# The order of high and low matmuls inside a unit: grouped for most columns, five orders for gate and up

## The reference

```python
# first block
proj = h @ w_in                      # mixer: SSD part, short convolution part
... @ w_out
q = (h @ w_q); k, v = mem_n @ w_k, mem_n @ w_v; ... @ w_o
(jax.nn.silu(h @ w_gate) * (h @ w_up)) @ w_down          # D_FF = 5632
# second block
p = h @ w_in[i]                      # pool, hyena and gated mixers
... @ w_out[i]
up = dwconv3(h @ ffn_w_up[i], ...); gate, val = jnp.split(up, 2, axis=-1)
x = x + (jax.nn.silu(gate) * val) @ ffn_w_down[i]
```

## Time and profile before

| | |
|---|---|
| median of 3 runs | 2719.59 us |
| profiled execution | 2724.14 us, of which the span of instructions 2722.4 us |
| TensorE busy | 2656.2 us, 98% of the span |
| VectorE, ScalarE busy | 1924.6 us, 1495.8 us |
| granted TensorE clock, mean | 0.992 |
| memory traffic | 490.76 MB, mean 180 GB/s |

### The profile page before, as it was taken

How to read it: one execution, slowest core, us unless ns; L and a number is a source line. 1 busy time by engine, 2 the same in 40 slices (tenths; PEclk the granted TensorE clock), 3 DMA queues, 4 the chain that set the end, 5 groups by cost and what they waited for, 6 DMA issues and landing times.

```text
span 2722.4 us, 38546 instructions
## 1 busy us (share of the span) xinstructions
PE 2656.2 (98%) x14978; PEld 2286.7 (84%) x14978; DVE 1924.6 (71%) x2916; ACT 1495.8 (55%) x2307; POOL 388.7 (14%) x391
## 2 busy tenths in 40 slices
PE   7999999999998999999999999999999999999997
PEld 7888888888887888888888878888888888888886
DVE  8776777777787665656565679687876767676775
ACT  6555566768555444444444456545555555555554
POOL 3011100403411000010101033011101010101012
PEclk9999999999998999999999999999999999999998
DMA  6555566656554555666666656536566666666663
GB/s 247 173 180 182 184 191 193 186 182 183 174 175 134 168 162 171 186 187 188 189 186 187 190 161 209 162 124 185 178 193 188 187 189 189 186 187 187 190 178 118
DMA packets 135838, 490.76 MB, mean 180 GB/s; under 512 B 15207, under 2 KB 15528, under 8 KB 135656
## 3 DMA queue, kind: packets, MB, share of 16 engines
q1 hardware_dynamic: 135656, 488.31, 59.2%
HBM read 486.12 MB, written 2.13 MB: 179 GB/s over the span
## 4 chain that ended last, share of the span: by engine, by line
PE 87%; DVE 8%; ACT 2%; issue 2%; DMA 0%; DVEq 0%; ACTq 0%; SPq 0%
PE ps L715 32%; PE ps L733 24%; PE ps L716 16%; PE ps L730 12%; DVE wl L1218 3%; ACT wh L936 1%; DVE hT L1218 1%; DVE X L1224 1%; PE ps L872 0%; PE ps L905 0%; DVE A L1224 0%; DVE T L1224 0%; DVE R L1218 0%; DVE Gf L1218 0%; DVE T L1218 0%
## 5 line engine op out<-in xcount | busy, mean ns | idle before, releaser
L1218 DVE TENSOR_TENSOR wl<-raw,wh 128x1024 fp32r<-128x1024 f32 x902 | 1139.7, 1268 | 723.9 <-ACT wh L936 722.6
L936 ACT ACTIVATE wh<-raw 128x1024 fp32r<-128x1024 f32 x902 | 952.4, 1059 | 967.2 <-PE ps L716 536.2
L733 PE MATMUL ps<-X,wh 128*128 128x512 f32 x2816 | 860.1, 396 | 2.8 <-DVE hT L1218 2.8
L715 PE MATMUL ps<-XG,wh 128*128 128x512 f32 x2304 | 827.3, 403 | 29.7 <-DVE hT L1218 16.4
L715 PE MATMUL ps<-X,wh 128*128 128x512 f32 x2032 | 725.2, 401 | 2.0 <-DVE wl L1218 1.3
L716 PE MATMUL ps<-XG,wl 128*128 128x256 f32 x2304 | 650.4, 282 | 0.0
L716 PE MATMUL ps<-X,wl 128*128 128x256 f32 x2032 | 568.7, 280 | 0.0
L730 PE MATMUL ps<-X,wl 128*128 128x256 f32 x2816 | 564.6, 281 | 0.0
L715 PEld LDWEIGHTS ps<-XG,wh 128*128 128x128 f32 x2304 | 436.8, 190 | 142.9 <-DVE hT L1218 21.8
L733 PEld LDWEIGHTS ps<-X,wh 128*128 128x128 f32 x2816 | 481.5, 189 | 71.9 <-issue 4.7
L730 PEld LDWEIGHTS ps<-X,wl 128*128 128x128 f32 x2816 | 484.6, 189 | 61.5
(11 more groups left out here) (172 smaller groups left out, 1313.6 us busy)
## 6 DMA issues: line engine op xcount, KB each, us to landing
raw<-in_w_gate SPq DMA_DIRECT2D x176, 512.0 KB, 3.7
raw<-in_w_down SPq DMA_DIRECT2D x176, 512.0 KB, 3.7
raw<-in_w_sc SPq DMA_DIRECT2D x96, 512.0 KB, 4.2
raw<-in_w_up SPq DMA_DIRECT2D x88, 512.0 KB, 3.7
raw<-in_w_val SPq DMA_DIRECT2D x88, 512.0 KB, 3.7
raw<-in_w_zx SPq DMA_DIRECT2D x80, 512.0 KB, 3.8
raw<-in_w_in SPq DMA_DIRECT2D x68, 512.0 KB, 3.8
raw<-in_w_osc SPq DMA_DIRECT2D x32, 512.0 KB, 3.7
```

The costliest lines, as they stand in the source:

```text
L715: e.matmul(bank(c, i)[:, :], W1, x, start=st and kk == 0, stop=False)
L733: t = e.matmul(bank(c, i)[:, :], wh[:, b0:b0 + 128], X[:, kx * 512:kx * 512 + 512], start=st and kk == 0, stop=sp and n == ends[i])
L936: return e.activation(out, in_, ACT.Copy, scale=scale)
L1218: return e.tensor_tensor(out, a, b, op)
```

## The change

The code that orders matmuls is written anew. Columns other than gate and up: for each k tile H for i = 0 and 1, then L for i = 0 and 1 (the v columns as before). Gate and up: `ORDERS` becomes the function `orders(which, first)`, picked by the same string of digits. Its five orders are: 0, the grouped H H L L, which was index 1's; 1, H and L in turn all through, each L on the other output tile than the H before it, first H(0) with L(1) and, from the middle, H(1) with L(0) (the first unit of a column starts with H H L, since each bank has to be begun by an H); 2, H(0) H(1) L(1) L(0) for each k; 3, for two k tiles each H H L H L H L L; 4, H H L, then H and L in turn, and an L last. Gate and up units wait for each of their four X tiles instead of once for the last, all ahead of the unit's first matmul. The other engines are as before.

```diff
--- before.py
+++ after.py
@@ -383,14 +383,25 @@
     return at
 
 
-
-ORDERS = [
-    [(k, i, m) for k in range(4) for i in range(2) for m in range(2)],
-    [(k, i, m) for k in range(4) for m in range(2) for i in range(2)],
-    [(k, i, m) for k in range(4) for i, m in ((0, 0), (0, 1), (1, 0), (1, 1))[:2] + (((1, 0), (1, 1)) if k == 0 else ((1, 1), (1, 0)))],
-    [(k, i, m) for m in range(2) for k in range(4) for i in range(2)],
-    [(k, i, m) for q in range(2) for m in range(2) for k in (2 * q, 2 * q + 1) for i in range(2)],
-]
+def orders(which, first):
+
+
+    if which == 0:
+        return [(k, i, m) for k in range(4) for m in range(2) for i in range(2)]
+    if which == 1:
+        head = [(0, 0, 0), (0, 1, 0), (0, 1, 1)] if first else [(0, 0, 0), (0, 1, 1)]
+        mid = [(0, 0, 1)] if first else [(0, 1, 0), (0, 0, 1)]
+        return (head + [(k, i, i) for k in range(1, 4) for i in range(2)] + mid +
+                [(k, 1 - m, m) for k in range(1, 4) for m in range(2)])
+    if which == 2:
+        return [(k, i, m) for k in range(4) for i, m in ((0, 0), (1, 0), (1, 1), (0, 1))]
+    if which == 3:
+        return [(k, i, m) for k in (0, 2) for k, i, m in ((k, 0, 0), (k, 1, 0), (k, 0, 1), (k + 1, 0, 0), (k, 1, 1), (k + 1, 1, 0),
+                                                         (k + 1, 0, 1), (k + 1, 1, 1))]
+    return [(0, 0, 0), (0, 1, 0), (0, 0, 1)] + [(k - (i and m), i, m) for k in range(1, 4) for i, m in (
+        (0, 0), (1, 1), (1, 0), (0, 1))] + [(3, 1, 1)]
+
+
 ORDER_OF = [int(d) for d in "0123401324" "0214303142" "10432042" "0123412034" "431021"]
 
 PLAN = schedule()
@@ -703,25 +714,26 @@
             st, sp = u == c.first, u == c.last
             for kk in range(c.kn):
                 X, kx, s, n = xtile(c, g * c.kn + kk)
-                if kk == 0 or c.kind not in ("gate", "up"):
-                    w.wait_ge(s, xtile(c, g * c.kn + c.kn - 1)[3] if c.kind in ("gate", "up") else n)
-                x = X[:, kx * 512:(kx + 1) * 512]
+                w.wait_ge(s, n)
                 if c.kind in ("gate", "up"):
                     continue
-                for i in range(nb):
-                    b0 = (u % NW) * UN + kk * c.w
-                    if c.kind != "v":
-                        W1, W2 = wh[:, b0 + 128 * i:b0 + 128 * i + 128], wl[:, b0 + 128 * i:b0 + 128 * i + 128]
-                        e.matmul(bank(c, i)[:, :], W1, x, start=st and kk == 0, stop=False)
-                        t = e.matmul(bank(c, i)[:, 0:256], W2, x[:, 0:256], start=False, stop=sp and kk == c.kn - 1)
-                    else:
-                        W1, W2 = wh[:, b0:b0 + 256], wl[:, b0:b0 + 256]
+                x = X[:, kx * 512:(kx + 1) * 512]
+                b0 = (u % NW) * UN + kk * c.w
+                if c.kind == "v":
+                    W1, W2 = wh[:, b0:b0 + 256], wl[:, b0:b0 + 256]
+                    for i in range(2):
                         xh, xl = x[:, i * 128:i * 128 + 128], x[:, 256 + i * 128:384 + i * 128]
                         e.matmul(bank(c, i)[:, 0:256], xh, W1, start=st and kk == 0, stop=False)
                         e.matmul(bank(c, i)[:, 0:256], xh, W2, start=False, stop=False)
                         t = e.matmul(bank(c, i)[:, 0:256], xl, W1, start=False, stop=sp and kk == c.kn - 1)
+                else:
+                    for i in range(nb):
+                        e.matmul(bank(c, i)[:, :], wh[:, b0 + 128 * i:b0 + 128 * i + 128], x, start=st and kk == 0, stop=False)
+                    for i in range(nb):
+                        t = e.matmul(bank(c, i)[:, 0:256], wl[:, b0 + 128 * i:b0 + 128 * i + 128], x[:, 0:256], start=False,
+                                     stop=sp and kk == c.kn - 1)
             if c.kind in ("gate", "up"):
-                order = ORDERS[ORDER_OF[c.i]]
+                order = orders(ORDER_OF[c.i], st)
                 ends = {i: n for n, (kk, i, low) in enumerate(order)}
                 for n, (kk, i, low) in enumerate(order):
                     X, kx = xtile(c, g * c.kn + kk)[:2]
```

## The result

The changed kernel takes 2710.43 us (median of 7 runs, 2708.15 to 2715.05), the kernel before 2719.28 (median of 7, 2717.61 to 2724.88). The ratio is 0.9969 with a 95% interval of 0.9958 to 0.9980: 8.4 us less, between 5.4 and 11.4. The forecast was 2709.5, with 2702 to 2717 as its range.

What follows compares the result with a forecast made beforehand. TensorE's pace of starting matmuls was taken as the bound. Other columns -10.2 us and gate and up +0.1 gave -10.1: 2714.0 from the profiled 2724.1, or 2709.5 from the median 2719.6, the forecast; range 2702 to 2717.

Steps and rivals of the forecast that it cites:

- 249 x 0.040: Undisturbed units outside gate and up at 2.827 us go to 2.787 when grouped: -10.0 us.
- The 118 fast units: Undisturbed units outside gate and up at 2.773 us lose 0.014 each when grouped: +1.6 us.
- The 57 units behind pieces: Units outside gate and up starting after a small piece of other matmuls, 2.902 to 2.887 us each: -0.9 us.
- The 83 long units: Units outside gate and up containing waits or long pieces: taken as -0.3 us, bounds 0 and -3.3.
- Gate and up: All five orders of the gate and up columns together: +0.1 us, ends about -9 and +6.
- Index 1: 72 gate and up units going from grouped to strict turns, 2.787 to 2.810 us each: +1.6 us.
- Index 3: 64 gate and up units, half grouped and half alternating, 2.794 to 2.807 us each: +0.8 us, ends -1.3 and +2.1.
- The rival that the usual execution holds fewer slow units than the profiled one: Timed executions may hold 84 slow units fewer, so grouping wins 4.5 us less: -5.6 us, 2714.0; chance 0.16.
- a wait for wl above 13.9 us: Sign of being wrong: TensorE idle ahead of L731 for split weights grows, the split on ScalarE and VectorE bounding next.
- All new orders at the floor: Rival: gate and up index 1 to 4 all run at 2.773 us a unit, -18.9 us in all, 2701; chance 0.11.
- Order worth nothing outside gate and up: Rival: elsewhere the pace is set by something that comes along, such as the X buffer read: 2719.6 us; chance 0.05.
- A price for the turn of banks: Rival: an L following an H into another bank costs 0.07 us or more a unit in index 1, 3, 4; chance 0.05.

Runs made afterwards that it cites:

- the other columns alone: Kernel before with only the columns other than gate and up put in H H L L, gate and up keeping their five old orders: 2712.03 us, ratio 0.9961.
- All grouped: Changed kernel with every column in H H L L, gate and up too: 2709.61 us, 0.9954 of the kernel before; timed again 2707.91 us, 0.9950.
- All pairwise: Kernel before with every column in H L H L, gate and up too: median 2718.93 us, ratio 1.0002 to the kernel before.
- the two bank patterns of index 1: Changed kernel against one whose index 1 units send each L to the same bank as the H before it; the latter took 2716.17 us, one execution.

## Why the prediction was right

**The bound and the quantity.** That TensorE's pace sets the time, and that the start-to-start distance of a unit is what to read, held in every run: VectorE, ScalarE and the memory queues did the same work throughout, while the time moved between 2700.7 and 2718.9 with the sequence alone.

**Other columns.** The term that carries the forecast, 249 x 0.040, came out as -10.0, and grouped units stood at 2.787 in the changed kernel and in every experiment that kept them. The 118 fast units cost a little more than +1.6, since some met waits. The 57 units behind pieces gave +0.4 instead of -0.9, but one of them (at 93.59 after) ran at the lower clock and added 1.6; without it they gave -1.2, and -1.1 with the other columns alone grouped, so the size is right. The name of the group was too narrow: of the 66 units of 2.85 to 2.94 us, counted from first start to the next matmul, only 35 follow a piece directly.

**Units with waits.** The 83 long units were put at -0.3 with a bound of -3.3; they measured -5.3, outside the bound. Six of them, the last four w_o units and those at 711.16 and 1571.29, ran, or waited behind a unit that ran, at the lower clock before; they gave -6.1, and the other 77 cost 0.8 more. The bound had assumed an equal clock. This is also why the spans fell by 13.8 us and the times by 8.4: the one profiled execution of each kernel was not equally lucky. All grouped had a clock of 0.94 in 740 to 861 in one profile and 0.97 in the other, so the order does not set it.

**Gate and up.** Forecast +0.1, measured +1.1 without the three disturbed units of index 0. Index 0, 2 and 4 were within 0.3 us. Index 1 came to +1.3 for +1.6, but for another reason than given: I had let TensorE fall into the slow pace in 68 of 100 units by chance; in truth, in seven of nine pairs, the gate column is slow and the up column fast, because the first unit of each column, with its H H and its L L, moves TensorE to the other pace. Index 3 was mis-sized: taken as 2.807, halfway, it is 2.826, near the end of its bound, +1.9 for +0.8. An average of neighbours was no model for it: the sequence keeps TensorE near its slowest pace.

**From the span to the time.** I subtracted from the median and not from the profiled execution, because that one had been 4.5 us above. That was right in size. The rival that the usual execution holds fewer slow units than the profiled one isn't needed for the gap, which goes with the clock: of 22 executions of the kernel before, the five with a granted clock of 0.992 over the whole execution took 2722.5 us in the mean and the three with 0.995 took 2716.6; the profiled one had 0.992. Nor does the profiler add the time, which the prediction held possible: the profiled execution of the changed kernel, 2710.43, is its median. All pairwise does show clusters at equal clock, so such a state exists; for the kernel before none is shown.

**How much was luck.** At an equal clock the trace gives -7.5 us and not -10.1. Most of the 2.6 us between them are index 3 and the long units, which each cost about 1 us more than was put down for them, and the fast units (0.7). The interval of the times, -5.4 to -11.4, holds both numbers, so that the median came to 0.9 us of the forecast is in part luck. One of the signs of being wrong was a wait for wl above 13.9 us: it was 14.6, with the same single wait of 12.6 in it, so the split did not become the bound.

**The rivals.** All new orders at the floor: no, only the up columns of index 1 were. Order worth nothing outside gate and up: refuted by the other columns alone, 0.9961. A price for the turn of banks: none, the two bank patterns of index 1 agree to 0.01 us a column, and those of index 0 and 2 stand at 2.787 both. The rule that the prediction took from the Trainium skill ("TensorE: Matmul & The Clock Gate", section "Back-to-back issue gap") would have put every kernel here at the same time, since all issue the same matmuls. The runs disagree: 2700.7 to 2718.9 us. That section gives the formula for an isolated matmul and says that in a stream the weight loads set the spacing too; "whatever stood before it" was the prediction's own reading of it.

**What stays open.** What the two states are inside TensorE. The trace of all pairwise shows their form. In the fast stretch of 232 units the starts of H are 343 and 350 ns apart in turn, two pairs in 693 or 694 ns; in the slow stretch of 184 units they are 350, 361 and 349 ns apart, three pairs in 1060 ns, but for three places in 1467. A unit has eight pairs, so the slow rhythm fits only after three units, which is the slow cycle of 2.831, 2.819 and 2.830 us. The weight loads last 187 to 190 ns in both stretches, so their length doesn't part the paces; whether their timing does was not tried. The units of the several orders stand at 2.773, 2.780, 2.787, 2.794, 2.800, 2.807, 2.820 and 2.827 us, as if in steps of some 7 ns; nothing here shows why. Which disturbance leaves which pace was not tried either.

## What to carry to other kernels

When TensorE is the bound and its busy share says 98%, measure the distance between the starts of matmuls over whole units, per sequence and per stretch: a few per cent can hide there, and the busy time does not show them. An order of long and short matmuls can have more than one steady pace for the same instructions; judge it by all its stretches, and judge an order also by the pace in which it leaves the code behind it. A pattern that is never at its best but has one pace (H H L L) is the choice where other work breaks in; one that can lock into the best pace pays where nothing does, if it is entered by a sequence that leads there. And compare the clock of the short stretches before believing the difference of two spans.

## What was unexpected of the hardware

- Strict turns of a 512-column and a 256-column matmul run at 0.3467 us a pair or at 0.3533, at a granted clock of 1.00, for over 180 units on end, with no instruction changed: a rhythm of two pairs in 693 ns, or of three in 1060 ns.
- Grouped turns (H H L L) have only 2.787 us a unit; runs of eight equal matmuls are no better (2.794), and runs of four are worse (2.807). The fewest changes between long and short is not the best order.
- A short break in the turns moves TensorE between the paces, and the move depends on the sequence and on the place of entry in a slow cycle of three units (2.831, 2.819, 2.830): HHLL twice keeps fast, HHLL once leaves it, and HHLL, HL four times, HHLL keeps it, at a price of 0.047 us, and reaches it from some places only.
- The PSUM bank that a matmul adds to, the same as the one before or another, makes no difference that can be measured: in turns of H and L 11.30 or 11.31 and 11.12 us a column, in grouped units 2.787 us a unit either way.
